# Two-layer transformer pair on one core: modulation columns in pairs, a low-rank product moved back, and a norm factor applied after the product

## The reference

```python
def first_block(x, c, ...):
    c_act = jax.nn.silu(c)
    for l in range(2):
        mod = (c_act @ w_ada[l] + b_ada[l])[:, None, :]          # 6 x 1024
        shift_m, scale_m, gate_m, shift_f, scale_f, gate_f = jnp.split(mod, 6, axis=-1)
        h = rms_norm(x, norm_mix[l]) * (1.0 + scale_m) + shift_m
        x = x + gate_m * hybrid_mixer(h, ...)       # 8 stick-breaking heads, 4 gated linear heads
        h = rms_norm(x, norm_ffn[l]) * (1.0 + scale_f) + shift_f
        x = x + gate_f * hierarchical_moe(h, ...)   # 32 experts, top 2 of one group
    return x

def second_block(x, ...):
    for l in range(2):
        h = rms_norm_2(x, norm1_g[l])
        ...                                          # four branches: y_a (MLA), y_b (diff), y_c (window), y_d (neighbours)
        mix = jnp.concatenate([rms_norm_2(y_a, out_g_mla[l]), y_b,
                               rms_norm_2(y_c, out_g_swa[l]), rms_norm_2(y_d, out_g_na[l])], axis=-1)
        x = x + mix @ w_out[l]
        h = rms_norm_2(x, norm2_g[l])
        x = x + jnp.square(jax.nn.relu(h @ w_up[l])) @ w_down[l]
    return rms_norm_2(x, final_norm_g)
```

## Time and profile before

| | us |
|---|---|
| median of 3 runs | 1699.75 (1699.04 to 1701.88) |
| profiled execution, device time | 1698.64 |
| its span in the profile | 1696.8 |
| TensorE busy | 1616.9 |
| VectorE busy | 1175.3 |
| ScalarE busy | 927.8 |
| mean granted TensorE clock | 0.985 |

### The profile page before, as it was taken

One profiled execution on the slowest core, in us unless ns is written; L12 is line 12 of the kernel. 1 busy time (PEld: TensorE's weight loads), 2 busy tenths in 40 slices (PEclk: granted clock), 3 DMA queues, 4 the chain that ended last, 5 costly groups with the idle time before them and its releaser, 6 DMA issues.

```text
span 1696.8 us, 24960 instructions
## 1 busy us (share of the span) xinstructions
PE 1616.9 (95%) x10392; PEld 1385.3 (82%) x10392; DVE 1175.3 (69%) x1380; ACT 927.8 (55%) x1192; POOL 99.1 (6%) x68
## 2 busy tenths in 40 slices
PE   6999989999999999899999998998999999989997
PEld 3676779999996687699999987777999886879996
DVE  2644578999997635879999987685545586755554
ACT  3361457777776442477777765365444454544442
POOL 0200000101010200000110101100000011000000
PEclk9999999999999999999999999999999999989999
DMA  9768728999996766259999995052665532435551
GB/s 329 281 228 297 261 77 337 349 370 346 374 346 226 253 213 248 99 194 373 347 361 358 350 348 132 19 198 91 205 203 184 168 93 99 150 100 195 181 195 63
DMA packets 132534, 392.12 MB, mean 231 GB/s; under 512 B 23360, under 2 KB 36672, under 8 KB 107840
## 3 DMA queue, kind: packets, MB, share of 16 engines
q1 hardware_dynamic: 131840, 388.35, 64.5%
q10 hardware_dynamic: 576, 2.10, 0.4%
HBM read 389.37 MB, written 1.05 MB: 230 GB/s over the span
## 4 chain that ended last, share of the span: by engine, by line
PE 86%; DVE 6%; ACT 3%; POOL 2%; DMA 1%; issue 1%; SPq 0%; POOLq 0%; ACTq 0%; DVEq 0%
PE ps L1169 19%; PE ps L473 12%; PE ps L2150 10%; PE ps L1194 9%; PE ps L453 5%; PE ps L1648 4%; PE ps L1672 3%; PE ps L516 2%; PE ps L641 2%; PE ps L532 2%; PE ps L1624 2%; PE ps L1693 2%; PE ps L1708 1%; POOL hh L1409 1%; DVE spl L369 1%
## 5 line engine op out<-in xcount | busy, mean ns | idle before, releaser
L369 DVE TENSOR_TENSOR spl<-ring,spl 128x2048 fp32r<-128x2048 f32 x255 | 592.3, 2325 | 184.2 <-ACT spl L360 183.9
L360 ACT ACTIVATE spl<-ring 128x2048 fp32r<-128x2048 f32 x254 | 486.8, 1917 | 179.0 <-PE ps L473 107.7
L1169 PE MATMUL ps<-spl,ur 128*128 128x256 f32 x3072 | 370.7, 280 | 1.2 <-DVE ur L1392 1.2
L1169 PEld LDWEIGHTS ps<-spl,ur 128*128 128x128 f32 x3072 | 359.3, 190 | 2.4 <-DVE ur L1392 2.0
L473 PEld LDWEIGHTS ps<-hh,spl 128*128 128x128 f32 x1728 | 205.2, 190 | 7.7 <-issue 5.9
L473 PE MATMUL ps<-hh,spl 128*128 128x256 f32 x1728 | 207.4, 281 | 2.8 <-DVE hh L436 2.8
L1194 PE MATMUL ps<-spl,hh 128*128 128x512 f32 x768 | 186.6, 392 | 2.1 <-DVE hh L1363 2.1
L2150 PE MATMUL ps<-spl,ur 128*128 128x512 f32 x768 | 176.7, 389 | 0.0
L815 DVE TENSOR_TENSOR spl<-ring,spl 128x1024 fp32r<-128x1024 f32 (+2 forms) x126 | 144.9, 1176 | 37.9 <-ACT spl L806 37.0
L806 ACT ACTIVATE spl<-ring 128x1024 fp32r<-128x1024 f32 (+2 forms) x128 | 124.4, 1016 | 78.7 <-PE ps L453 23.9
L2150 PEld LDWEIGHTS ps<-spl,ur 128*128 128x128 f32 x768 | 143.2, 188 | 29.2
(11 more groups left out here) (360 smaller groups left out, 1746.1 us busy)
## 6 DMA issues: line engine op xcount, KB each, us to landing
ring<-in_w_up SPq DMA_DIRECT2D x96, 1024.0 KB, 5.3
ring<-in_w_down SPq DMA_DIRECT2D x96, 1024.0 KB, 5.1
ring<-in_w_gate SPq DMA_DIRECT2D x64, 1024.0 KB, 5.0
ring<-in_w_ada SPq DMA_DIRECT2D x48, 1024.0 KB, 7.1
ring<-in_w_in SPq DMA_DIRECT2D x34, 1024.0 KB, 7.7
ring<-in_w_out SPq DMA_DIRECT2D x16, 1024.0 KB, 7.7
ring<-in_w_in SPq DMA_DIRECT2D x8, 384.0 KB, 3.4
gate<-in_b_ada ACTq DMA_DIRECT2D x4, 512.0 KB, 5.7
```

The source lines that it names most:

```text
L360: sc.activation(t.hi, t.raw, ACT.Copy).then_inc(s_hi, 2)
L369: v.tensor_tensor(t.lo, t.raw, t.hi, ALU.subtract).then_inc(s_lo, 1)
L1169: ins = pe.matmul(ps[:, 2 + e % 2, 256 * z:256 * z + 256], le, ri, start=(k == 0 and j == 0 and z == 0), stop=(k == 7 and j == 2), skip_gr ...
```

## The change

1. **Pairs.** A shift or scale is now formed from both its blocks at once. Block c is summed and copied to the first half of a scratch, then, after a wait for that copy, block c+1 is summed in the same bank and copied to the second half, and one move of eight products takes both (128 columns instead of 64 as the stationary operand). VectorE adds and multiplies once, on 128 partitions. The scratch of the lane is `gate[:, 1, :]`. So the bias of gate_f can't be loaded there at the start of the mixer: SyncE loads it ahead of the first output tile, behind a wait for the last pair's move. The two gate_f blocks come last in the lane, in layer 0 behind blocks 0 to 3 of layer 1 (and the tiles are loaded in that order). In the prologue the sums of blocks 0 and 1 come first, then the transposes, the sum of block 2, the move of blocks 0 and 1, the sum of block 3, the move of blocks 2 and 3.
2. **Low-rank product.** In layer 0, TensorE runs it behind the first projection's first tile (three steps of lane 0), not ahead of it.
3. **Late factor.** Branch D of the second mixer is transposed unscaled. The last output tile goes to banks of its own, `OD = (3, 4, 5, 7)`. VectorE adds the four banks `OB` once the third tile is done, then adds the banks `OD` times the row factor, which ScalarE computes after it has written the high part.
4. **Orders** of both first mixers on all three engines, and VectorE's in the second mixers (one step of branch D fewer).

By the orders, TensorE's steps in layer 0 begin, after the change: `in` 0 three steps, low-rank, `in` 0 last step, the gate's product L686, two steps of `in` 1, a modulation sum, a step of `in` 1, query transposes. Before: low-rank, four steps of `in` 0, L686, two steps of `in` 1, query transposes. They end, after: the last pair's move, the last step of `in` 5, sum, sum and move of block 10, sum, sum and move of block 11, the gated heads' transposes, eight output steps. Before, with blocks (1, 2) and (1, 3) at the end: the last step of `in` 5, move of (1, 2), two sums, the first output step, the transposes, move of (1, 3), seven output steps. In layer 1 the second output step of the gated heads moves from ahead of the first output step to behind it.

```diff
-ORDER = {("mix1", 0, "PE"): "400004006650505055066501235501231521325515123125501231502352505055045045540505540450455450455055504450000000",
+ORDER = {("mix1", 0, "PE"): "00040400506650505506650123551023123123550121321325101252505505040455405505455404504504505555554400000000",
...
-            blocks = [(l, c) for c in range(4, 12)] + [(1, c) for c in range(4) if l == 0]
+            blocks = [(l, c) for c in range(4, 10)] + [(1, c) for c in range(4) if l == 0] + [(l, 10), (l, 11)]
...
+        PAIRS = [(0, 0), (0, 2)]
+        for _l in range(2):
+            PAIRS += [(_l, 4), (_l, 5), (_l, 6), (_l, 8)] + [(1, 0), (1, 2)] * (_l == 0) + [(_l, 10), (_l, 11)]
+        ada_n = {p: n for n, p in enumerate(PAIRS)}
...
         def pe_ada_move(pe, l, c, bank, e):
-            s, h = divmod(c, 2)
-            pe.wait_ge(s_ev, ada_n[l, c] + 1)
-            if s in (2, 5):
+            pe.wait_ge(s_ev, ada_copies(l, c))
+            if ada_pair(l, c):
+                for k in range(8):
+                    ins = pe.matmul(ps[:, bank, k:k + 1], e[:, :, k::8], C("ones")[:, 0:1], start=True, stop=True)
+            else:
                 ins = pe.matmul(ps[:, bank, :], C("ones"), e, start=True, stop=True)
-            else:
-                for k in range(8):
-                    ins = pe.matmul(ps[64 * h:64 * h + 64, bank, k:k + 1], e[:, k::8], C("ones")[:, 0:1], start=True, stop=True)
...
                 run(pe_ada_sum(pe, 0, 1, 5))
                 pe.wait_ge(s_ld, 32)
-                pe_ada_move(pe, 0, 0, 4, ev[1])
...
             if l == 0:
                 run(pe_ada_sum(pe, 0, 2, 6))
-                pe_ada_move(pe, 0, 1, 5, ev[2])
+                pe_ada_move(pe, 0, 0, 4, ev[1])
                 run(pe_ada_sum(pe, 0, 3, 7))
-                pe_ada_move(pe, 0, 2, 6, ev[3])
-                pe_ada_move(pe, 0, 3, 7, ev[4])
+                pe_ada_move(pe, 0, 2, 6, ev[2])
...
                 yield from pe_ada_sum(pe, al, c, 7)
-                pe_ada_move(pe, al, c, 7, ev[0])
+                if ada_pair(al, c):
+                    pe.wait_ge(s_ev, ada_copies(al, c) - 1)
+                    yield from pe_ada_sum(pe, al, c + 1, 7)
+                pe_ada_move(pe, al, c, 7, ev[3] if ada_pair(al, c) else ev[0])
                 yield
...
             pe.wait_ge(s_staged, 4 * l + 4)
+            if l == 0:
+                pe.wait_ge(s_used, T["in", 0, 0, 0].m + 1)
...
-            for q, s in ((0, 2), (1, 5)):
-                sc.dma_start(gate[:, q, :], a["b_ada"][l, s * 1024:(s + 1) * 1024].partition_broadcast(128)).then_inc(s_gb, 16)
+            sc.dma_start(gate[:, 0, :], a["b_ada"][l, 2048:3072].partition_broadcast(128)).then_inc(s_gb, 16)
...
-                                ins = pe.matmul(ps[:, OB[2 * c + i], :], le, ri, start=(t == 0 and kk == 0 and q == 0), stop=(t == 3 and kk == 1 and q == 2),
+                                ins = pe.matmul(ps[:, (OD if t == 3 else OB)[2 * c + i], :], le, ri, start=(t in (0, 3) and kk == 0 and q == 0),
+                                                stop=(t in (2, 3) and kk == 1 and q == 2),
...
-            yield from pe_fin2(pe, l, "D", V + 19)
+            yield from pe_fin2(pe, l, "D", None)
...
+            if scaled is None:
+                for s, n in units_done(br, l):
+                    pe.wait_ge(s, n)
...
         def act_fin2(sc, l, br, turned):
+            if br != "D":
+                act_factor2(sc, l, br)
+                yield
+            act_turned2(sc, l, br, turned)
+            yield
+            if br == "D":
+                act_factor2(sc, l, br)
+                yield
...
+            v.wait_ge(s_used, T["out2", l, 2].m + 1)
+            for c in range(2):
+                for i in range(2):
+                    xs = x[:, i, 512 * c:512 * c + 512]
+                    ins = v.tensor_tensor(xs, xs, ps[:, OB[2 * c + i], :], ALU.add)
+            v.wait_ge(*own_dve(ins))
+            v.wait_ge(a_ms, 13 * l + 13)
...
-                    dve_add(v, c, i, ps[:, OB[2 * c + i], :], None)
+                    xs = x[:, i, 512 * c:512 * c + 512]
+                    v.scalar_tensor_tensor(xs, ps[:, OD[2 * c + i], :], st[:, 208 + i:209 + i], xs, ALU.mult, ALU.add).then_inc(s_x, 1)
...
+                for l in range(2):
+                    if t is T["out", l, 0]:
+                        sy.wait_ge(s_adp, ada_n[l, 10])
+                        sy.dma_start(gate[:, 1, :], a["b_ada"][l, 5120:6144].partition_broadcast(128)).then_inc(s_gf, 16)
```

More of the change, by code:

```diff
@@ L837, in act_ada_lane @@
             for al, c in ada_blocks(l):
-                act_ada(sc, al, c, 7, ev[0])
-                yield
+                if not ada_pair(al, c):
+                    act_ada(sc, al, c, 7, ev[0])
+                    yield
+                    continue
+                for h in range(2):
+                    act_ada(sc, al, c + h, 7, ev[3][:, h, :])
+                    yield
         def act_gla(sc, l):
@@ L900, in dve_mix1 @@
             if l == 0:
-                for c in range(4):
+                for c in (0, 2):
                     dve_ada(v, 0, c, 4 + c)
@@ L1712, in pe_misc2 @@
         def pe_misc2(pe, l):
-            A, V = 13 * l, 20 * l
+            A, V = 13 * l, 19 * l
             r = slice(64, 96)
```

65 lines of the change are left out of this document (36 added, 29 removed), and 6 rows, old and new, of the table ORDER.

## The result

| | before | after |
|---|---|---|
| median of the runs, us | 1700.82 (1699.04 to 1703.48, 4 runs) | 1716.78 (1713.65 to 1719.62, 4 runs) |
| ratio after/before | | 1.0087, 95% interval 1.0064 to 1.0110 |
| profiled execution / its span, us | 1698.64 / 1696.8 | 1714.35 / 1712.6 |

What follows compares the result with a forecast made beforehand. TensorE's queue, busy 95% of the span, plus its idle and slow stretches was taken as the bound. Layer 0 +7.8, layer 1 -0.5 and late factor -5.0 gave +2.3 us; forecast 1701.5 us, range 1692 to 1709.

Steps and rivals of the forecast that it cites:

- The price of a strided load: Modulation moves: 0.21 to 0.25 us per 128-column load, 3.65 us a pair against 4.0 for two singles; -1.5 us in layer 0.
- rival B: Modulation moves: a load costs per instruction, not per column, so each pair costs 2.0 us; 1684 us in all; chance 0.08.
- The clock falls: After pair moves in the first mixers: 85% followed by a fall of 1.4 us; +4.8 us layer 0, -0.7 layer 1.
- rival A: First mixers: the clock falls no more often after pairs than after singles; 7.2 us less, 1694.3 us; chance 0.20.
- The low-rank product: Layer 0's first mixer: standing in line behind the first projection tile costs +3.6 us, with -1.7 for the projection's earlier start.
- cold first tile: Layer 0's first projection tile starts after some 8 us of idleness at 1.2 GHz; +2.0 us, between 0 and 2.7.
- The query transposes: Layer 0's first mixer: a modulation sum and projection step ahead of them cover TensorE's wait on the norm chain; -1.9 us.
- rival C: First projection of layer 0: SyncE's DMA ring starves behind the low-rank weights' slot; +3 to +10 us, 1707.5; chance 0.25.
- The late factor: Branch D of both second mixers: output tile 2.33 us earlier, plus 0.2 us of clock each; -5.0 us for two layers.
- rival D: Second mixers: the late factor does not shorten because another wait ends where it did; +5 us, 1706.5; chance 0.05.
- the tail: End of layer 0's first mixer: gate blocks' exposed waits against work paid earlier; +1.5 us, bounds -2 to +4.
- only 8.3 us of output products now lie between: +0.9: End of layer 1's first mixer: VectorE's 9.15 us chain is covered by only 8.3 us of output products; +0.9 us.

Runs made afterwards that it cites:

- the mended waits: Changed kernel with layer 1's first-mixer ends reordered, one weight tile's split kept inside VectorE's gated chain and the other put later; 1716.4 us, ratio 1.0085.
- both mended orders: Changed kernel with two reorderings of the end of layer 1's first mixer, differing in where VectorE splits the output weights; 1719.3 and 1716.4 us.
- the fastest kernel: Kernel before plus late factor, with contiguous single-block moves and its old first-mixer orders; 1678.8 us, ratio 0.9870.
- the ends of layer 1: Changed kernel with the second head-output step before the first output product and VectorE's gated product before a weight split, in layer 1's first mixer; 1719.3 us.
- the end of layer 0: Changed kernel with only TensorE's last steps of layer 0's first mixer reordered around the FFN gate blocks; 1722.1 us, ratio 1.0122.
- the kernel of all mended parts: Changed kernel with contiguous pair moves, low-rank product in front and layer 1's first-mixer ends reordered; 1691.1 us, ratio 0.9948.

## Why the prediction was wrong, and where it was right

**Right.** The price of a strided load: 3.65 us a move forecast, 3.85 measured, so rival B (per instruction) was false. That it came so near is in part luck. The row that it leaned on, 16 loads in 4.01 us, belongs to products of 512 moving columns, which come 0.23 us apart over adjacent loads too (48 in 11.18 us above); that row alone couldn't give a price. The durations of single loads in the same trace could have: 0.33 us at every eighth element (L1162), 0.19 adjacent (L1142). And 32 loads in 3.49 us are 0.109 us each, not 0.105. The clock falls: 85% forecast, six of six measured, and rival A was false. The low-rank product: 3.63 us in line. The first projection: 44.84 us against a forecast 44.4, the difference being the prologue (+1.4, forecast +1.0); cold first tile +1.4 (forecast +2.0). The query transposes follow at 71.66 without a wait (-1.9). The ring (rival C) did not starve. The late factor: -2.77 us at the tile in each layer (forecast -2.33), -5.5 in all with the clock against -5.0, and rival D was false.

**Wrong, layer 0 (+12.4, forecast +7.8).** Two terms of the sum were mis-sized. *Clock falls after pairs*: +4.8 was the price for four falls at 1.4 us. They cost 1.7 each of dense work, and the first stretch was twice as long (119.4 to 126.2 us): 8.5 in the lane against 1.5 before, of which some 0.3 lies in a move, +6.7. *Moves*: -0.7 in place of -1.5, since they took 3.85 and not 3.65. With the terms that held (1.4 - 1.7 + 3.6 - 1.9 + 1.4) that makes +8.8. The remaining 3.6 belong to *the tail*, forecast +1.5, and to the head steps, which I had at nothing: 1.4 us of new waits there (L769, L764), and between the last projection step and the output products 0.72 + 0.83 + 1.29 + 1.36 = 4.2 us of waits where 1.3 stood. That is 4.3 in new waits, 0.7 more than is missing, and I can't place the difference. I had seen the tail's waits and held against them the work that leaves the stretch; that work is paid earlier, the waits are new.

**Wrong, layer 1 (+7.0, forecast -0.5).** The term that failed is "only 8.3 us of output products now lie between: +0.9". It took the chain's 9.15 us from the earlier trace rows and only shortened the cover. The new order strings of VectorE also put a split into the chain: 11.4 us against 8.4 of cover is the wait of 3.35, and the second wait grew from 1.50 to 2.06. Then the clock fell over the last 48 products: +2.3. That the waits were the reason is not shown: it fell there with the mended waits (0.78 + 1.29 + 1.50) too, and not before, with 1.50 alone. That makes 6.2 where 0.9 stood. Another 0.6 is the query norm wait (2.45 after 1.85), the two falls after moves cost the same as the two before and not 0.7 less, and the moves gave 0.2, not 0.7: 7.1 of the 7.5 missed. The step left out was to walk VectorE's new order through the chain as I had walked TensorE's. That an order alone doesn't win the 6 us back, both mended orders showed.

**Not in the sum at all:** the first expert stage, +1.8. Its code is unchanged; its first gather took 5.75 us in place of 4.33 at a clock of 0.57. Which idle moments are followed by a fall there changes from kernel to kernel: at this gather or within 30 us of it there is a fall in 12 of the 16 traces, and none in that of the fastest kernel. The stage took 318.3 us in the changed kernel, and 316.8, 317.0 and 318.0 in three kernels with the same first mixer of layer 0 ahead of it, against 316.4 before and 316.7 with the late factor alone: most of the +1.8 is chance and not a price of the change. I called such phases a risk and priced them at nothing.

Together 4.6 + 1.8 + 7.5 - 0.5 = 13.4 us, which is the step from the forecast +2.3 to +15.7. The slow clock is about half of it: 12.3 us more than before in the trace, where the sum had 5.7 (4.8 + 2.0 - 0.7 - 0.4). None of my rivals had it; the slower one was the DMA ring.

## What to carry to other kernels

Before merging small products to save TensorE instructions, look at the layout of what they load: here the copy that stood ahead could write it contiguously at no cost, which halved each move (2.01 to 1.09 us), and merging two of them then saves 0.2 us. The kernel with single blocks and the orders of before beat every kernel with pairs; how much of that is the pairs, the gate blocks at the end of the lane, the late bias or the orders was not taken apart. Judge a stretch of one-column products by what comes behind it: the slow clock took 12.3 of the 15.7 us lost, and the stretches of 3.6 to 4.1 us were followed by a fall in 41 of 42 cases. When order strings are rewritten, follow each chain through the order of every engine in it; two of the mends here (the ends of layer 1, the end of layer 0) only moved a wait, because the order of another engine, or a later step of the same one, stood in the way.

## What the runs showed of the hardware

At the 2.4 GHz level a weight load of 128 columns with one moving column costs 0.115 us if the columns are adjacent and 0.24 at every eighth fp32 element; of 64 columns 0.065 to 0.068 and 0.125. The Trainium skill (TensorE: Matmul & The Clock Gate, LDWEIGHTS) gives P/1.2 ns, by estimate 107 and 53 ns: the contiguous rows agree to within some 10 to 30%, the strided ones don't. My prediction had used it only to say that width alone saves nothing; it saves 0.2 us a pair in either layout.

At the 1.2 GHz level the adjacent load costs nearly twice as much and the strided one the same. Rows: a contiguous pair's move of the prologue in the kernel of all mended parts and the windows view around it, then the window around the changed kernel's strided move at 32.72, 3.96 us like the one at 116.08:

```profile
31.30 3.58 PE L546 MATMUL ps<-cst,ar 128*128 128x1 f32 x16 [0.72 <-ACT ar L540]
31.30:34.90 3.60, 3.58 (x16) 0.50 1.11 342
...
32.70:36.70 4.00, 3.96 (x16) 0.50 1.04 314
```

So the stride doubles a load at 2.4 GHz (0.115 to 0.24 us) and adds a tenth at 1.2 GHz (0.22 to 0.24), and a strided move that falls into a slow stretch pays nothing for it.

The granted clock fell to 1.2 GHz behind stretches in which TensorE was never idle by the profile. Behind lane moves of 3.7 to 4.0 us it did so in 36 of 36 cases (six kernels with the strided pair), behind 3.6 to 4.1 us without stride in 5 of 6, behind 1.8 to 2.1 us as told above. A fall cost 1.7 us where the work behind it was dense, some twice that.
